# The down projection of a decoder layer by seven block products for eight of its twelve column pairs, with one set of raw weights

## What is computed

```
D_FF = ((8 * D_MODEL // 3 + 255) // 256) * 256          # 2816
...
        hn = rmsnorm(h, norm_ffn[layer])
        h = h + (jax.nn.silu(hn @ w_gate[layer]) * (hn @ w_up[layer])) @ w_down[layer]
    return rmsnorm(h, norm_final)
```

## Time and profile before

| | |
|---|---|
| median of 3 runs | 2235.14 us (2235.04 to 2236.0) |
| the profiled execution | 2236.66 us, its span 2234.9 us |
| mean granted PE clock | 0.994 of full |
| PE busy | 98% of the span |
| DVE, ACT, POOL busy | 50%, 41%, 31% |
| first down-projection matmul | at 1974.5 us |
| last down-projection matmul | at 2220.6 us |

### The profile page before, as it was taken

One profiled execution on the slowest core, in us unless ns is written; L12 is line 12 of the kernel. 1 busy time (PEld: TensorE's weight loads), 2 busy tenths in 40 slices (PEclk: granted clock), 3 DMA queues, 4 the chain that ended last, 5 costly groups with the idle time before them and its releaser, 6 DMA issues.

```text
span 2234.9 us, 30780 instructions
## 1 busy us (share of the span) xinstructions
PE 2185.5 (98%) x11040; PEld 1823.1 (82%) x11040; DVE 1113.3 (50%) x1559; ACT 918.5 (41%) x1627; POOL 693.5 (31%) x529
## 2 busy tenths in 40 slices
PE   6999999999999999999999999999999999999998
PEld 4788788887877888888888888888888888878887
DVE  7621423314257656655665544434866666650054
ACT  5644444443345555555554542123433333330013
POOL 6885665656531111111111114421000000043340
PEclk8999999999999999999999999999999999999999
DMA  5112213213231211211211344241222222261221
GB/s 134 50 48 67 86 57 86 66 48 105 80 92 47 66 38 47 66 38 47 66 57 37 132 146 128 84 124 29 79 81 81 78 81 79 84 233 50 76 76 76
DMA packets 251922, 175.66 MB, mean 79 GB/s; under 512 B 41448, under 2 KB 225960, under 8 KB 251840
## 3 DMA queue, kind: packets, MB, share of 16 engines
q1 hardware_dynamic: 221776, 136.46, 20.9%
q10 hardware_dynamic: 30064, 38.10, 5.3%
HBM read 143.36 MB, written 31.18 MB: 78 GB/s over the span
## 4 chain that ended last, share of the span: by engine, by line
PE 86%; DVE 3%; ACT 3%; issue 2%; POOL 2%; DMA 1%; POOLq 1%; ACTq 1%; DVEq 0%; SPq 0%
PE bank L213 20%; PE bank L2272 17%; PE bank L1064 15%; PE bank L2523 10%; PE bank L1277 6%; PE bank L1527 2%; PE bank L1510 2%; PE bank L687 1%; PE bank L2288 1%; DMA raw_first<-in_w_in 1%; PE bank L1517 1%; PE bank L698 1%; PE bank L1564 1%; DVE own_sum_t L486 1%; POOL q_lo_s L941 1%
## 5 line engine op out<-in xcount | busy, mean ns | idle before, releaser
L213 PE MATMUL bank<-u_hi,w_hi 128*128 128x512 f32 x704 | 311.0, 442 | 3.2 <-ACT z_next L1749 3.0
L199 POOL CAST w_hi<-raw 128x1024 fp32r<-128x1024 f32 (+1 forms) x60 | 61.1, 1018 | 707.2 <-PE bank L213 484.1
L213 PE MATMUL bank<-u_hi,w_lo 128*128 128x512 f32 x704 | 276.9, 393 | 0.0
L213 PE MATMUL bank<-u_lo,w_hi 128*128 128x512 f32 x704 | 276.3, 393 | 0.0
L2504 POOL CAST dn_hi<-dn_raw 128x896 fp32r<-128x896 f32 (+1 forms) x24 | 24.8, 1031 | 564.5 <-DMA dn_raw<-in_w_down 458.9
L213 PEld LDWEIGHTS bank<-u_hi,w_lo 128*128 128x128 f32 x704 | 132.4, 188 | 29.0
L201 POOL TENSOR_TENSOR w_lo<-raw,w_hi 128x1024 fp32r<-128x1024 f32 (+1 forms) x60 | 150.7, 2512 | 8.6
L213 PEld LDWEIGHTS bank<-u_hi,w_hi 128*128 128x128 f32 x704 | 134.0, 190 | 19.1 <-ACT z_next L1749 3.4
L213 PEld LDWEIGHTS bank<-u_lo,w_hi 128*128 128x128 f32 x704 | 134.0, 190 | 15.0 <-issue 1.9
L941 POOL TENSOR_TENSOR q_lo_s<-q_sum_s,q_hi_s 128x512 fp32r<-128x512 f32 x92 | 122.2, 1334 | 74.7 <-ACT q_hi_s L996 69.1
L1817 DVE SCALAR_TENSOR_TENSOR conv_out<-conv_in,conv_c,conv_out 128x1024 f32<-128x1024 f32 (+1 forms) x96 | 100.3, 1045 | 15.0 <-issue 12.0
(11 more groups left out here) (433 smaller groups left out, 5856.9 us busy)
## 6 DMA issues: line engine op xcount, KB each, us to landing
raw<-in_w_in SPq DMA_DIRECT2D x36, 512.0 KB, 3.9
raw_first<-in_w_in SPq DMA_DIRECT2D x24, 512.0 KB, 4.0
raw_second<-in_w_in SPq DMA_DIRECT2D x24, 512.0 KB, 4.9
row<-scr_rows ACTq DMA_DIRECT2D x24, 512.0 KB, 4.6
raw_gate<-in_w_gate SPq DMA_DIRECT2D x22, 512.0 KB, 3.8
raw_up<-in_w_up SPq DMA_DIRECT2D x22, 512.0 KB, 3.8
scr_v<-gate_out SPq DMA_DIRECT2D x44, 256.0 KB, 2.1
tmp<-scr_gate ACTq DMA_DIRECT2D x16, 512.0 KB, 3.7
```

Source lines behind the costliest of these rows:

```text
L199: nc.gpsimd.tensor_copy(hi[:, 0:kt, :], raw[slot][:, 0:kt, :])
L213: last = nc.tensor.matmul(bank[dst][:, :], wpart[slot][wp][:, k, :], rhs[ap][:, k, half * HALF:(half + 1) * HALF], start=k == 0 and (wp, a ...
```

## The change

The down projection is now done like the stage before it, by 2x2 block products. v has three chunks (`KH`: halves of 3, 4 and 4 k tiles, so 6, 8 and 8 k tiles), and each chunk goes through the four pairs of column tiles: pairs 0 to 11 in all, numbered n. Pairs 0, 4, 8 and 11 keep eight block products (`PLAIN`), the eight others have seven (`PRODUCTS`), each with its own result taken out by DVE: seven additions to `h_t` in place of four.

The operand blocks of a chunk are loaded once each (x11, x21, x12, x22, and x11 and x21 a second time into the buffers where t1 and t4 are formed). DVE forms t1 to t4 and all low parts of operands; ACT casts them. The weights of a pair come in two transfers into one set of raw buffers (`raw_gate`, `raw_up`, left from the stage before). ACT casts the weight blocks, POOL forms the sums s1 to s4 and all low parts. SP asks for the weights of pair n when all low parts of pair n - 1 have been written. In the pairs after a plain pair, POOL forms s1, s2 and s4 ahead of the low parts of s2 and s1. A block of pair n may be written when PE has finished the product of pair n - 1 that used its place.

```diff
@@ -2381,8 +2381,8 @@
                 for i in range(7):
                     up_step_act(act, NFF // 2 - 1, b, i, last=b == 1)
-                    if b == 1 and i >= 3:
-                        v_cast(act, i - 3)
+                    if b == 1:
+                        first_chunk_act(act, i)
...
+        KH, V_ROW = (3, 4, 4), (0, 6, 14)
+        NDN = 4 * len(KH)
+        LAST_UP = 7 * (NFF - 1)
+        PLAIN = (("a", "x11", 0, 0), ("c", "x21", 0, 0), ("b", "x11", 1, 0), ("d", "x21", 1, 0),
+                 ("b", "x12", 1, 1), ("a", "x12", 0, 1), ("d", "x22", 1, 1), ("c", "x22", 0, 1))
+        PLAIN_ADD = ((2, 0, 0), (4, 1, 0), (7, 1, 1), (8, 0, 1))
+        SEVEN_ADD = ((0, 0), (0, 0), (0, 1), (1, 1), (1, 1), (0, 1), (1, 0))
+        SAME_BEFORE = {1: 1, 4: 4, 5: 3}
+        PLAIN_FREE = {"b": 5, "a": 6, "d": 7, "c": 8}
+        PLAIN_BANKS = ((X0, X1), (Z0, Z1))
+        SEVEN_BANKS = {1: (D0, D1), 2: (Y0, Y1), 3: (D0, D1)}
...
+        V_LOADS = (("x11", 0, 0), ("x21", 1, 0), ("x12", 0, 1), ("t1", 0, 0), ("x22", 1, 1), ("t4", 1, 0))
+        V_FREED = (1, 2, 3, 4, 6, 7)
...
+        def is_plain(n):
+            return n % 4 == 0 or n == NDN - 1
...
+        def load_part(sp, n, i):
...
+                sp.wait_ge(dn["low"], PARTS_BEFORE[n])
+            kt, row = 2 * KH[c], V_ROW[c] * P
+            sp.dma_start(dn_raw[i][:, 0:kt, :], w_cols(w_down[0][row:row + kt * P, :], (2 * fp + i) * P, kt)).then_inc(loaded(n, i)[0], 16)
...
+                for i, (o, _, _) in enumerate(V_LOADS):
+                    load_v(sp, c, o, (up["done"], LAST_UP + V_FREED[i]) if c == 0 else (dn["done"], DONE_BEFORE[last] + V_FREED[i]))
+                    if c and i == 0:
+                        load_part(sp, 4 * c, 0)
+                        load_part(sp, 4 * c, 1)
+                    if o == "x22":
+                        load_part(sp, 4 * c + 1, 0)
+                        load_part(sp, 4 * c + 1, 1)
+                for n in range(4 * c + 2, 4 * c + 4):
+                    load_part(sp, n, 0)
+                    load_part(sp, n, 1)
+                    if n == 2:
+                        up_store(sp, NFF // 2 - 1, 1)
...
+            def total(n, name, first, second, op):
+                wait_place(pool, n, name)
+                g.tensor_tensor(part_sum(n, name), first, second, op).then_inc(dn["sum"], 1)
+                pool.drain()
+
+            for n in range(NDN):
+                pool.wait_ge(*loaded(n, 0))
+                if is_plain(n):
+                    pool.wait_ge(*loaded(n, 1))
+                    for name in low_order(n):
+                        low(n, name)
+                    continue
...
+                low(n, "c")
+                pool.wait_ge(*loaded(n, 1))
+                total(n, "s1", part_raw(n, "b"), part_raw(n, "d"), ALU.add)
+                total(n, "s2", part_sum(n, "s1"), part_raw(n, "a"), ALU.subtract)
+                if n % 4 == 1:
+                    total(n, "s4", part_raw(n, "c"), part_sum(n, "s2"), ALU.subtract)
+                    low(n, "s2")
+                    low(n, "s1")
+                    total(n, "s3", part_raw(n, "a"), part_raw(n, "b"), ALU.subtract)
+                    low(n, "s3")
+                else:
+                    low(n, "s1")
+                    total(n, "s3", part_raw(n, "a"), part_raw(n, "b"), ALU.subtract)
+                    low(n, "s3")
+                    total(n, "s4", part_raw(n, "c"), part_sum(n, "s2"), ALU.subtract)
+                    low(n, "s2")
+                low(n, "s4")
+                low(n, "d")
...
+            first, second = {"t1": ("x12", "t1"), "t3": ("x22", "x12"), "t2": ("x22", "t1"), "t4": ("t4", "t2")}[o]
...
+                for m, (name, o, side_) in enumerate(PRODUCTS):
+                    pe.wait_ge(dn["low"], low_at(n, name))
+                    if fp == 1:
+                        pe.wait_ge(v_low_done, V_LOW_BEFORE + 8 * c + V_OPERAND[o])
+                    if m > 1:
+                        pe.wait_ge(dn["added"], ADDED_BEFORE[n] + m - 1)
+                    for kk in range(kh):
+                        last = product(n, bank[SEVEN_BANKS[fp][side_]][:, :], name, o, kk, kh, m in (0, 1, 3), True)
+                    last.then_inc(dn["done"], 1)
...
+        def next_chunk_vec(dve, c, m):
+
+            if m == 4:
+                v_low(dve, c, "x11")
+            elif m == 5:
+                v_low(dve, c, "x21")
+            elif m == 6:
+                v_sum(dve, c, "t1")
+                v_sum(dve, c, "t3")
+                v_low(dve, c, "x12")
+                v_sum(dve, c, "t2")
+                v_low(dve, c, "x22")
...
+                if is_plain(n):
+                    for j, (done_, i, half) in enumerate(PLAIN_ADD):
+                        down_add(dve, n, i, half, PLAIN_BANKS[i][half], done_)
+                        if j == 0:
+                            v_low(dve, c, "t1")
+                        elif j == 1:
+                            v_sum(dve, c, "t4")
+                            v_low(dve, c, "t2")
+                        elif j == 2:
+                            v_low(dve, c, "t3")
+                    continue
...
+                for m, (i, half) in enumerate(SEVEN_ADD):
+                    down_add(dve, n, i, half, SEVEN_BANKS[fp][PRODUCTS[m][2]], m + 1, SAME_BEFORE.get(m, 0))
+                    if fp == 1 and m == 0:
+                        v_low(dve, c, "t4")
+                    if fp == 3:
+                        next_chunk_vec(dve, c + 1, m)
+                    if c == 2 and m >= 3:
+                        final_sum_vec(dve, fp - 1, *FINAL_OUT[m - 3], m - 3)
+                    if n == NDN - 2 and m == 5:
+                        v_low(dve, 2, "x12", True)
...
+                elif is_plain(n):
+                    v_cast(act, c, "x22")
+                    part_cast(act, n + 1, "a")
+                    part_cast(act, n + 1, "c")
+                    v_cast(act, c, "t1")
+                    for name in ("s1", "s2", "s4"):
+                        part_cast(act, n + 1, name)
+                    v_cast(act, c, "t2")
+                    part_cast(act, n + 1, "s3")
+                    v_cast(act, c, "t3")
+                    part_cast(act, n + 1, "d")
+                    v_cast(act, c, "t4")
```

More of the change, by code:

```diff
@@ L2440, in build @@
[L2440 to L2447, removed]
@@ new lines, in build @@
+        SUMS_BEFORE = [4 * sum(not is_plain(m) for m in range(n)) for n in range(NDN + 1)]
+        DONE_BEFORE = [sum(8 if is_plain(m) else 7 for m in range(n)) for n in range(NDN + 1)]
+        ADDED_BEFORE = [sum(4 if is_plain(m) else 7 for m in range(n)) for n in range(NDN + 1)]
+        dn = {x_: sem("dn_" + x_) for x_ in ("done", "added", "sum", "high", "low")}
+        v_summed, v_high_done, v_low_done = ba_split, ba_done, ba_turned
+        V_SUM_BEFORE, V_HIGH_BEFORE, V_LOW_BEFORE = 1, 2, NCH
@@ L2520, in down_pe, with product @@
         def down_pe(pe):
-            def product(n, i, half, g, part, k, k0, end, first):
+            def product(n, dst, name, o, kk, kh, start, stop):
                 for wp, ap in PASSES:
-                    last = nc.tensor.matmul(bank[DN_BANKS[g % 2][i][half]][:, :], dn_part[(n + i) % 4][wp][:, k, :],
-                                            (v_hi, v_lo)[ap][(k0 + k) // 2][:, (k0 + k) % 2 * 2 + half, :],
-                                            start=first and (wp, ap) == PASSES[0], stop=end[1] and (wp, ap) == PASSES[-1])
-                if end[0]:
-                    last.then_inc(dn["done"], 1)
@@ L2529, in down_pe @@
[L2529 to L2532 removed]
+                    last = nc.tensor.matmul(dst, (dn_hi, dn_lo)[wp][place_of(n, name)][:, kk, :], (t_hi, t_lo)[ap][o][:, kk, :],
+                                            start=start and kk == 0 and (wp, ap) == PASSES[0],
+                                            stop=stop and kk == kh - 1 and (wp, ap) == PASSES[-1], skip_group_check=True)
@@ L2601, in build, with down_add @@
-        f_sum = at("f_sum", [P, S], F32, T_AT["t4"])
-        f_now = at("f_now", [P, S], F32, T_AT["t4"] + 4096)
-        f_rms = at("f_rms", [P, KT], F32, T_AT["t4"] + 8192)
+        def down_add(dve, n, i, half, src, done_, same=0):
+            dve.wait_ge(dn["done"], DONE_BEFORE[n] + done_)
+            wait(dve, dn["added"], ADDED_BEFORE[n] + same if same else 0)
+            hf = h_t[:, 2 * (n % 4) + i, half * HALF:(half + 1) * HALF]
+            nc.vector.tensor_tensor(hf, hf, bank[src][:, :], ALU.add).then_inc(dn["added"], 1)
```

391 lines of the change are left out of this document (251 added, 140 removed).

## The result

The changed kernel takes 2256.68 us (median of 4 runs, 2255.49 to 2257.55), the kernel before on the same chip 2235.57 (4 runs, 2235.04 to 2237.72). The ratio is 1.0089, 95% interval 1.0078 to 1.0101: slower by 21.1 us, where 19.4 and a median of 2254 were forecast. The profiled execution took 2257.55 us, span 2255.8.

What follows compares the result with a forecast made beforehand. The prediction took the number of down-projection matmuls as the bound. Matmuls -19.7, old waits -2.3, new waits +37.5 and clock +3.9 sum to +19.4 us, a median of about 2254 us, range 2238 to 2266.

Steps and rivals of the forecast that it cites:

- 87 matmuls less, 0.2267 us each: Down projection: seven-block pairs drop 87 of 1056 matmuls, at their full-clock spacing, for -19.7 us.
- DVE and GpSimd take turns; 2048 with 512 is 3.3 us: Operand preparation: two-input operations on DVE and POOL alternate by whole instruction; a 2048 and a 512 together cost 3.3 us.
- The signs named ahead: Down projection: PE idle 30 to 45 us, most at pairs 5 and 9's third product; POOL's 512 near 2, DVE's 2048 near 2.8.
- The first rival: DVE and POOL pass each other at their own lengths, leaving about 9 us of small waits: 2222 us, 12% chance.
- Pairs 0 and 1, 8.2 us: First chunk: PE waits 5.6 us for c's low part in pair 1, 1.2 in pair 0 and 1.4 later.
- Up to pair 5, 16.5: Second chunk's start: PE waits 2.1 and 3.1 us for x11 and x21, about 9.5 at pair 5's third product, 1.8 elsewhere.
- The third rival: Columns of pairs 5 and 9 take 13 us, their chains end up to 5 us later: 2262 to 2270, 13% chance.
- Pairs 8 and 9, 10.9: Third chunk's start repeats pairs 4 and 5 with columns on time: waits of 0.6 and 10.3 us at the third product.
- around pair 11, 1.9: Last pair of the down projection: PE waits 1.9 us because ACT's four squares stand ahead of casts.
- The clock, three drops at 1.3 us, +3.9: Behind three waits over 3.8 us PE runs 2.8 us at 1.2 GHz, +3.9 us in all, bounds 0 to +6.
- As many bytes: Transfers: columns and operands move as many bytes as before, so this term is 0.
- any waits under 22 us: Down projection: with PE's waits under 22 us in all, the change was said to pay.

Runs made afterwards that it cites:

- e1: Changed kernel with each of GpSimd's sums and weight low parts replaced by two memsets that read nothing (blocks zero); 2219.22 us.
- e3: Changed kernel with 30 extra matmuls on TensorE ahead of the wait for the third product of pairs 5 and 9; 2253.94 us.
- e6: Changed kernel with a second raw weight set, t3's low part behind the first addition, and ACT's cast of pair 0's block d two copies later; 2237.89 us.
- f1: e6 with DVE's low parts of t3 and t4 one addition later still in pairs 1, 5 and 9; 2234.75 us.
- f2: e9 with t3's low part behind the second addition and t4's behind the fourth; 2234.56 us.
- e9: e6 with ACT's casts of t2 and t3 ahead of those of s4 and s3 in pairs 5 and 9; 2236.05 us.
- f3: Changed kernel with each of GpSimd's sums and weight low parts replaced by two copies reading one SBUF input; 2264.48 us.
- e4: Changed kernel with DVE's low part of t3 moved behind the first addition of pairs 1, 5 and 9; 2252.72 us.
- e5: Changed kernel with a second raw weight set, pair n's columns asked for when pair n-2's last low part is done; 2251.78 us.
- e8: Changed kernel with ACT's cast of pair 0's block d two copies later, behind the up projection's gate_out copies; 2254.09 us.

## Why the prediction was right, point by point

- **87 matmuls less, 0.2267 us each.** Right: with no turns (e1) the stage and tail are 18.6 us shorter than before with 0.3 less of waits, where the spacing gives 20.0; e1's restarts and a few products of 2.8 to 2.9 us around pairs 4 and 5 take some of it back.
- **DVE and GpSimd take turns; 2048 with 512 is 3.3 us.** Right, 3.14 to 3.38 in pair 5, and shown by e1 to be what the whole loss hangs on. The signs named ahead are there: PE idle for 30.4 us with its largest pieces at the third product of pairs 5 and 9, POOL's 512 operations at a mean of 1.83 us, DVE's 2048 ones at 2.71. The first rival (they pass each other, 2222 us) is what e1 looks like at 2219. DVE's additions from a bank kept 682 ns.
- **Pairs 0 and 1, 8.2 us:** 6.6, with 5.25 at product c (5.6 forecast).
- **Up to pair 5, 16.5:** 13.9. x11 and x21 waited 1.04 and 1.58, not 2.1 and 3.1. Two steps failed. One is x11's low part, which I had held for a turn: it began 0.06 us ahead of POOL's subtraction, so it ran its own 2.29 us and POOL's was the one that was held (3.38, the two rows below). The other is x21's load behind two weight loads, which I had land 2.4 us into the pair and which ACT used at 0.8 (2048.23). The third product of pair 5 waited 9.15 (9.5), by the chain as written, t3's cast ending 36.2 us after PE could start pair 4 (38.1 forecast). The third rival did not come: POOL's low part of a, the first for pair 5, began 12.3 us in (2059.72), where 12.7 was forecast, so that pair's columns were on time.

```profile
2046.06 3.38 POOL L2574 TENSOR_TENSOR dn_lo_p<-raw_gate,dn_hi_p 128x512 fp32r<-128x512 f32 x1
```
```profile
2046.00 2.29 DVE L2650 TENSOR_TENSOR u_hi<-n_raw,u_hi 128x2048 fp32r<-128x2048 f32 x1 [1.96 <-ACT u_hi L2644]
```

- **Pairs 8 and 9, 10.9:** 9.2; **around pair 11, 1.9:** 0.8. All waits 30.4 instead of 37.5, every term a little high.
- **The clock, three drops at 1.3 us, +3.9.** The count was right, the size not. PE was busy at 1.2 GHz for 5.0 us behind 2001.8, 4.1 behind 2087.9 and 5.8 behind 2178.5, where I took 2.8 from the one stretch near the start. At 0.427 us a matmul in place of 0.2267 these 14.9 us lose 7.0, and the products there are 7.7 longer. The upper bound I gave, +6, was too low as well. With what the sum had no term for (restarts behind the short waits, and 1.6 without a row) it is +10.6. Only a part of it can be won back by itself, as e3 shows: of the 2.8 us won in two stretches 1.5 were waited away.
- **The start of the stage, nothing forecast:** the step that failed is that the waits begin with "1.2 in pair 0", with nothing ahead of it. I did not name what stood behind ACT's cast for pair 0 in its queue: the copies that free the up projection's banks. PE lost 1.1 us to that; the other 0.7 is open, and the start moves by some us between executions.
- **As many bytes.** Wrong, with no effect found: 6.8 MB more are read, as x11 and x21 are loaded again for t1 and t4 and x12 once more; the earlier trace rows had no row for it. Before and after:

```profile
HBM read 143.36 MB, written 31.18 MB: 78 GB/s over the span
...
HBM read 150.17 MB, written 31.18 MB: 80 GB/s over the span
```

Waits too high by 7.1 and clock, restarts, start and tail too low by 8.6 nearly cancel, so it is luck that 2254 is closer to 2256.7 than its terms are. The mechanism and the side do not rest on that luck. One bound of the text is wrong: the change does not pay with just any waits under 22 us. From the first matmul to the end, e6 with 14.4 us of waits is 2.1 longer than the kernel before, f1 with 13.8 is 0.8 shorter, f2 with 15.1 is 2.4 shorter and e9 with 17.2 is 1.5 longer. So even waits of about 15 us only break even; the 22 left out the low clock and the restarts that come with waits.

## What to carry to other kernels

Before arithmetic is traded for preparation, count the preparing instructions that read SBUF on DVE with two inputs and on GpSimd at the same time: each of GpSimd's can then be held for an operation of DVE on top of its own length. More and shorter instructions on GpSimd beside DVE were worse here (f3); fewer and longer ones were not tried. When several chains end at the same wait, single fixes can measure small (e4, e5 and e8 against e6); try them together before dropping them.

## What the runs showed of the hardware that was not expected

- GpSimd's copy with one SBUF input is held as a subtraction with two is: 0.62 us alone, 2.40 to 2.67 beside DVE's 2048-wide subtractions. Its memset is not held: 0.53 us, with DVE at 2.28.
- In pair 4 the engine that started second was the one held: DVE's subtraction that began 0.06 us ahead of GpSimd's took its own 2.29 us, GpSimd's 3.38.
- Behind waits of 9.15 and 8.74 us PE, busy without a break, ran 4.1 and 5.8 us at 1.2 GHz. In e3, where 30 extra matmuls had left 2.41 us of one of these waits, the clock did not drop.
